# Recurrence of a hybrid decoder layer: the lower products are laid out head by head in device memory

## The reference, cut to what matters

```
def step(state, inp):
    r_t, w_t, k_t, v_t, kk_t, a_t = inp
    sa = jnp.einsum('bhvk,bhk->bhv', state, -kk_t)
    state = (state * w_t[:, :, None, :]
             + sa[..., None] * (kk_t * a_t)[:, :, None, :]
             + v_t[..., None] * k_t[:, :, None, :])
    return state, jnp.einsum('bhvk,bhk->bhv', state, r_t)
_, y = lax.scan(step, state0, scan_in)
```

## Time and profile before

| | us |
|---|---|
| median of 3 runs | 3047.03 (3042.70 to 3053.33) |
| the profiled execution's own time | 3056.69 |
| its span, first to last instruction | 3055.1 |
| PE busy | 2764.1 (90%) |
| DVE busy | 1098.7 (36%) |
| POOL busy | 515.7 (17%) |

### The profile page before, as it was taken

The page is one execution under the profiler, slowest core; times in us unless marked ns, Lnnn a source line. Parts: engine busy times, 40 slices in busy tenths (PEclk is TensorE's granted clock), DMA queues, the critical chain, the costliest instruction groups (busy, mean ns, idle before and its releaser), DMA issues. The chain is left out here.

```text
span 3055.1 us, 51012 instructions
## 1 busy us (share of the span) xinstructions
PE 2764.1 (90%) x19900; PEld 2602.1 (85%) x19901; DVE 1098.7 (36%) x2466; ACT 652.3 (21%) x1239; POOL 515.7 (17%) x745
## 2 busy tenths in 40 slices
PE   8998898699997898884999999999999999999980
PEld 7875686388887888884999999999999999999980
DVE  2108422356654404353222222323223232232328
ACT  3118513233322213220111111111111111111111
POOL 0000001333430000043211112121221211212114
PEclk9998999789988999887999999999999999999995
DMA  7110010000003010137888778888888888887867
GB/s 246 32 30 13 27 49 23 10 19 19 19 11 131 15 55 15 58 106 230 303 296 293 267 263 296 297 302 294 301 298 297 294 301 296 301 299 258 301 234 275
DMA packets 337379, 548.03 MB, mean 179 GB/s; under 512 B 41072, under 2 KB 117744, under 8 KB 337264
## 3 DMA queue, kind: packets, MB, share of 16 engines
q1 hardware_dynamic: 317936, 503.98, 48.2%
q0 software_dynamic: 19360, 42.87, 4.8%
HBM read 505.49 MB, written 41.31 MB: 179 GB/s over the span
## 5 line engine op out<-in xcount | busy, mean ns | idle before, releaser
L2382 PE MATMUL experts_up<-experts_xs,g_pieces 128*128 128x144 f32 (+1 forms) x8192 | 1035.3, 289 | 34.8 <-DVE experts_xs L2311 29.4
L2382 PEld LDWEIGHTS experts_up<-experts_xs,g_pieces 128*128 128x128 f32 x8192 | 1028.8, 197 | 41.2 <-issue 41.1
L2405 PE MATMUL experts_down<-experts_hs,g_across 128*128 128x144 f32 (+1 forms) x3072 | 389.2, 288 | 0.0
L2405 PEld LDWEIGHTS experts_down<-experts_hs,g_across 128*128 128x128 f32 x3072 | 386.1, 190 | 0.0
L2266 POOL DMA_INDIRECT experts_x<-h_rows,experts_index x198 | 191.7, 968 | 1103.4 <-DVE experts_xs L2311 1048.5
L2341 DVE TENSOR_SCALAR experts_glu<-experts_up,experts_bias 128x176 f32<-128x176 f32 x256 | 102.5, 400 | 678.8 <-PE experts_up L2382 678.8
L2291 ACT ACTIVATE experts_sig<-experts_glu 128x352 f32<-128x352 f32 x128 | 63.7, 497 | 971.6 <-DVE experts_lin L2343 971.6
L2298 ACT ACTIVATE experts_yT<-experts_down,experts_bias 128x176 f32<-128x176 f32 x256 | 101.2, 406 | 384.2 <-PE experts_down L2405 236.6
L2332 DVE COPY experts_bias<-g_bias 128x24 f32 x32 | 5.8, 182 | 391.9 <-ACT experts_yT L2298 391.9
L2394 PE MATMUL experts_down<-experts_hs,g_across 128*128 128x144 f32 (+1 forms) x1024 | 133.2, 288 | 0.0
L2394 PEld LDWEIGHTS experts_down<-experts_hs,g_across 128*128 128x128 f32 x1024 | 130.1, 190 | 0.0
(11 more groups left out here) (410 smaller groups left out, 4098.8 us busy)
## 6 DMA issues: line engine op xcount, KB each, us to landing
g_pieces<-in_w_dram SPq DMA_DIRECT2D x132, 2048.0 KB
g_across<-in_w_dram SPq DMA_DIRECT2D x64, 2048.0 KB, 9.5
y_rows<-experts_y SPq DMA_DIRECT2D x132, 192.0 KB, 3.8
g_across<-in_w_ckv_dram SPq DMA_DIRECT2D x8, 1024.0 KB, 9.9
h_raw<-in_w_in_dram SPq DMA_DIRECT2D x15, 512.0 KB, 3.8
m_u<-in_x_dram SPq DMA_DIRECT2D x8, 512.0 KB, 10.5
g_across<-in_w_in_dram SPq DMA_DIRECT2D x8, 512.0 KB, 3.9
lower_rows<-chunk_ab SPq DMA_DIRECT2D x8, 512.0 KB
```

What stands on the lines that cost most here:

```text
L2382: ins = pe.matmul(up[:, u % 4, l * N:l * N + w], raw[c][:, k, at:at + 255:2], xs[:, k, 0:w], start=(k == 0), stop=(k == 7), skip_group_che ...
L2405: ins = pe.matmul(down[:, n % 4, 0:w], raw[4 + n // 4][:, k, (n % 4) * P:(n % 4 + 1) * P], hs[:, k, 0:w], start=(k == 0), stop=(k == 7), s ...
```

## The change

`lower_rows` is now one flat tensor in which each head has its own area of 129 x 128 numbers. A head's 128 x 128 matrix fills the first 128 x 128 of them. The spare row makes the area eight times 16 x 129 numbers long, and 16 x 129 = 16 x 128 + 16 is the step from one diagonal block to the next, so that the 64 blocks of all heads begin at equal distances. `diagonal` is that view: 64 blocks of 16 rows of 16 numbers. Partition 8s+h of `block16` and `small` becomes partition 8h+s. `solved_rows` becomes head, token, column, so that partition 8h+s's 256 numbers lie in one piece there.

```
-    lower = nc.dram_tensor("lower_rows", [P, H, P], F32).ap()
-    solved = nc.dram_tensor("solved_rows", [P, H, SIDE], F32).ap()
+    flat = nc.dram_tensor("lower_rows", [H * (P + 1) * P], F32).ap()
+    lower = flat.rearrange("(h a) -> h a", h=H)[:, 0:P * P].rearrange("h (p c) -> p h c", c=P)
+    diagonal = flat.rearrange("(b a) -> b a", b=H * GROUPS)[:, 0:SIDE * P].rearrange("b (j c) -> b j c", c=P)[:, :, 0:SIDE]
+    solved = nc.dram_tensor("solved_rows", [H, P, SIDE], F32).ap()
...
                     sp.dma_start(lower, ab[:]).then_inc(lower_out, 16)
                     sp.wait_ge(lower_out, n * 16 + 16)
-                    for s in range(GROUPS):
-                        at = slice(s * SIDE, (s + 1) * SIDE)
-                        sp.dma_start(block16[s * H:(s + 1) * H], lower[at, :, at].rearrange("j h c -> h j c")).then_inc(block_in, 16)
+                    sp.dma_start(block16[:], diagonal).then_inc(block_in, 16)
                     sp.wait_ge(ahead_pool.sem, ahead_pool.value(f"row{SIDE - 2}", n))
                     if not first:
                         sp.wait_ge(dve_steps.sem, dve_steps.value("inv", n - 1))
-                    for s in range(GROUPS):
-                        at = slice(s * SIDE, (s + 1) * SIDE)
-                        sp.dma_start(solved[at, :, :].rearrange("r h c -> h r c"), small[s * H:(s + 1) * H]).then_inc(solved_out, 16)
-                    sp.wait_ge(solved_out, n * (16 * GROUPS) + 16 * GROUPS)
-                    sp.dma_start(compact[:], solved).then_inc(compact_in, 16)
+                    sp.dma_start(solved.rearrange("h (s r) c -> (h s) r c", r=SIDE), small[:]).then_inc(solved_out, 16)
+                    sp.wait_ge(solved_out, n * 16 + 16)
+                    sp.dma_start(compact[:], solved.rearrange("h p c -> p h c")).then_inc(compact_in, 16)
...
-                    pool.wait_ge(block_in, n * (16 * GROUPS) + 16 * GROUPS)
+                    pool.wait_ge(block_in, n * 16 + 16)
...
-                    pool.wait_ge(solved_out, n * (16 * GROUPS))
+                    pool.wait_ge(solved_out, n * 16)
```

## The result

The changed kernel takes 3010.53 us (median of six runs, 3005.48 to 3016.29) where the kernel before, on the same chip, takes 3044.86 (3038.54 to 3053.33). The ratio is 0.9887 with a 95% interval of 0.9868 to 0.9907: faster by 34.3 us. The forecast was 3024.2 with a range of 3011 to 3042.

A forecast was written before the change was run, and what follows sets the result against it. PE bounds the recurrence, busy 299.9 of 339 us. Chunk 0's 2.9, chunks 2 to 7's 12.85 and the clock's 7.1 sum to 22.85 us, taking 3056.7 to 3033.8, or 3024.2 for the median; range 3011 to 3042.

The forecast's parts named there:

- The relay: Four DMA transfers around POOL's solve in each chunk: 2.9 us shorter, the transfers going from 12.8 to 9.9 us.
- Lower out: Relay's first transfer, writing the lower products out: 0.9 us longer, as 512-byte pieces replace 4 KB ones.
- blocks in: Relay's transfer of diagonal blocks in: 4.28 to 2.4 us, 1.88 less, one DMA replacing eight issues.
- solved out: Relay's transfer of solved blocks out: 4.06 to 1.6 us, 2.46 less, one DMA replacing eight issues.
- compact: Relay's last transfer, fetching `compact` in: 0.56 us longer, 1024 pieces of 64 bytes replacing 128 of 512.
- a relay only 1 us shorter: Rival for the relay: the two DMAs of 1024 small pieces take some 3.4 us each; 3039 us, chance 0.17.
- The longer relay: Rival for the relay: price goes by the piece, serially, 1.0 us more on seven chunks; 3056 us, chance 0.07.
- Chunk 0: Recurrence's first chunk, PE gap 9.49 us: the whole relay is ahead of PE, so all 2.9 us come through.
- Chunk 1: Recurrence's second chunk: gain 0, since DVE's spread starts without a wait, its masks being later than the relay.
- Chunks 2 to 7, the wait: PE's six gaps for `inv`, 1.91 to 2.47 us: all closed by the shorter relay, 12.85 us in total.
- What it is shorter beyond that buys nothing there: Chunks 2 to 7: a relay 2.5 us shorter closes every PE gap; further shortening gains nothing.
- The clock: PE's granted clock falling behind the gaps in the recurrence: 0 to 14.2 us to regain, half taken, 7.1.

The follow-up runs named there:

- experiments 1 and 2: Kernel before with one DMA bringing the blocks in, solved blocks still out in eight: cut by head (first, 3055.0 us), by block position (second, 3047.9 us).
- e2: Kernel before with solved blocks out in one DMA and `compact` in by 64-byte pieces, lower out and blocks in as before: 3014.2 us.
- e4: Changed kernel with the solved blocks written out a second time, to a spare tensor, and waited for in each relay: 3017.9 us.
- e3b: Kernel before with 8 idle products on PE in each chunk's gap ahead of level 4: recurrence 307.9 us for 330.2, whole program 30 us longer.
- e3c: Kernel before with 12 idle products on PE in each chunk's gap ahead of level 4: 3030.5 us.
- experiment 1: Kernel before with `lower` out head by head, one DMA for blocks in, solved blocks out in eight DMAs cut by head: 3055.0 us, ratio 1.0031.
- experiment 3: Kernel before with solved blocks out in one DMA, `compact` in by 64-byte pieces, and eight DMAs bringing the blocks in: 3014.2 us.

## Why the prediction was right in kind and short in size

**The relay: right in sum, by terms that offset.** 9.92 us against 9.9. Lower out rose by 0.3 (put at 0.9), blocks in fell by 1.39 (1.88), solved out by 2.11 (2.46), compact rose by 0.29 (0.56). The pieces' price was bounded well: 25600 packets in the stretch, as put, and the DMA of the blocks, the dearest, is 1040 of them:

```profile
q1 hardware_dynamic: 25600, 5.77, 9.1%
...
q1 hardware_dynamic: 1040, 0.07, 24.1%
```

24.1% of 16 engines over 2.89 us are 10.7 ns a packet, the 10.6 of the earlier trace rows; a second pass over small pieces does not show here either. The rivals of a relay only 1 us shorter, or longer, fall with these rows. The longer relay, made in experiments 1 and 2, was slower by 0.3% when some 1.9 us longer, and not measurably so when 1.1 us longer, where the rival had put 9 us for 1.0.

**Chunk 0: put at 2.9, measured 0.** The gap did shrink, from 9.49 to 6.92 us, but the chunk took 49.92 us in both. The first level's products took 3.75 us for 3.40, the second's 3.00 where those of before took 2.00. PE's columns over the same seven microseconds, changed kernel first, then the one before:

```profile
613.00:620.00 7.00, 7.00 (x35) 0.52 0.00 0
```

```profile
613.00:620.00 7.00, 7.00 (x57) 0.87 0.01 2
```

PE is busy throughout in both, and does 35 against 57 product instructions: the clock came back later in the chunk that had started its products earlier, and took the gain. With the gap filled the chunk took 46.5. In e2 and e4, whose gaps were longer (7.99 and 8.82 us), it took 47.6 and 48.1; over the three profiles with before's relay and no products in the gap it took 48.9, 49.9 and 52.6, and over the two with the changed relay 49.9 and 49.8. So this term moves by some 2 to 4 us from one execution to the next, and 0 is not its mean. The step that failed is that all of a shorter gap comes through: the slow products behind it were left out.

**Chunk 1: put at 0, measured 7.1. A step that failed.** DVE did not wait for `compact` there because, in that execution, its masks had been held up by the stall on POOL's product. I read the row as room in the schedule and it was a disturbance. With the stall away (e3b, 38.08) chunk 1 is like the others and the shorter relay is worth 2.5 us; the other 4.6 were stall and clock.

**Chunks 2 to 7, the wait: put at 12.85, measured 15.6.** By e3b, the same relay as before at full clock, against the changed kernel: 2.53, 2.70, 2.60, 2.64, 2.47 and 2.67 us. The gap was taken as the most that a shorter relay can give, but most of the 2.9 us arrived. 14.06 of the 15.61 us lie between the chunk's start and level 4 (2.22 to 2.65 each). The other 1.55 lie behind it, 0.24 to 0.34 in each of chunks 2 to 6, where e3b's PE waits 0.26 us for DVE ahead of level 5 as well, and the changed kernel's does so once, for 0.20. "What it is shorter beyond that buys nothing there" is refuted by e2 too, whose remaining gap of 0.4 us gave back 0.85 to 1.03.

**The clock: "I take half, 7.1". The step that cost most.** In the two executions it is 330.16 - 307.91 = 22.25 us for the whole recurrence (before less e3b), of which 16.45 lie in chunks 2 to 7. By the other execution of the kernel before (319.7 us) it would be 11.8, so its size is that of the execution taken. Two things were wrong. Chunk 7 was compared with chunk 5 (30.48 us up to its solution) as though that were undisturbed; an undisturbed one takes 28.3 (e3b), so the excess was 6.1 and not 3.9. And all of it fell away, not half: with no gap left there was no fall in chunks 2 to 7, in this kernel, in e2 and in e4. A half was a compromise, and the doses show why it was a poor one. Take a fall to be level 4's first products at 2.46 us or more, where undisturbed ones take 2.05 at the most, and leave out the chunks with idle products and those whose masks were late by the stall. Behind gaps of 0 to 1.68 us there was none. Behind 1.77 to 2.50 us there were 15 in 20, in changing places. Behind 3.15 to 4.38 us there were 12 in 12. The price doesn't grow alike: eight of the 15 cost 4 us or more, one of the 12 did.

That the row behind the gap showed half clock with PE fully busy was the right thing to look at, and the same is seen in chunk 2 before (columns of the earlier trace rows):

```profile
697.00:707.00 10.00, 10.00 (x48) 10.00 (x48) 6.79 (x12) 3.04 (x7) 2.52 (x1) 0.50 0.00 0
```

**The sum.** Put: 2.9 + 0 + 12.85 + 7.1 = 22.85. Measured between the two profiles: 0 + 7.08 + 15.61 + 16.45 = 39.14, the recurrence's difference, with 5.7 outside it. The medians differ by 34.3: the profile of before was one with more falls than usual. Less the 16.9 that e3b gives to the shorter relay, some 17 us are left for the clock and the stall in the typical execution. That is a difference, but e3c comes near to measuring it by itself: before's relay, the clock kept in chunks 2 to 7, no stall in the expert stage, 3030.5 us, ratio 0.9947, 16 us (11 to 22 by its interval). The low end of the range, 3011, was built with all 14.2 us of the clock and 1.5 in chunk 0, but with nothing for chunk 1 and the gap as a cap on the wait.

## What to carry to other kernels

When a wait ahead of the bounding engine is closed, count the products behind it at the full clock as well: if the rows behind the gap show the low level, the gap costs that too, and here it went as a whole once the gap was short enough, not in proportion. Take the undisturbed length of a stage from an execution in which the gap is filled with idle products, not from its quietest neighbour. And before a stage is said to have room, look whether one of its short steps is ten times as long there as elsewhere, and whether the bounding engine waits for what stands behind that step.

## What the runs showed of the hardware that was not expected

- PE's clock level followed short gaps. With gaps ahead of level 4 of up to 1.68 us there was no fall; at 1.77 to 2.50 us falls came in most of the chunks of each profile of the kernel before, each of the large ones worth 4 to 6 us; at 3.15 to 4.38 us they came in every chunk, but all of them small except one. In a large one the clock stayed at 0.50 for ten microseconds in which PE was busy without a break.
- The issue time of a small DMA depended on the layout more than on bytes or pieces: 8 KB in 128 pieces took 0.36 us to issue as in the earlier trace rows, 0.61 on the way out with the source's partitions 8 apart, and 0.71 on the way out cut by head (experiment 1). Cut by head on the way in (experiment 3), it took 0.36 again. One DMA with eight times the pieces took 0.60. What in the layout sets it stays open.
- A DVE step of four or eight columns in SBUF that begins during POOL's 2.1 us product waits for its end (2.04 to 2.10 us for some 0.2), as a copy, as a product with a constant and as a product of two tensors.
- Eight more products in each chunk on PE made the program 30 us slower, by waits in the expert stage behind it; twelve and sixteen did not.
